# State-space heads taken two by two on both column halves of TensorE, the decay broadcast in one pass, another order on ScalarE and VectorE

## The reference

```
zxbcdt = u @ w_in                          # z 2048, x 2048, B 512, C 512, dt 32 columns
xbc = silu(causal_depthwise_conv(xbc, conv_w, conv_b))      # width 4
dt = softplus(dt + dt_bias); a = -exp(a_log); da = dt * a; xdt = xs * dt
a_cs = cumsum(da) inside a chunk of 128 positions
cb = C^T B per chunk and group
y_diag = (cb * exp(a_cs[l] - a_cs[s]), s <= l) @ xdt        # per head
states = B, decay_to_end, xdt -> per chunk; prev = scan over the 4 chunks
y_off = C @ prev * exp(a_cs)                                # per head
y = y_diag + y_off + d * xs;  y = y * silu(z);  y = rms_norm(y per group) * norm_w
out = y @ w_out
```

## Time and profile before

| what | value |
|---|---|
| median of the runs | 2882.8 us (2881.28 to 2891.03) |
| profiled execution, its own time | 2888.43 us |
| its span in the trace | 2886.6 us |
| mean granted TensorE clock | 0.988 of full speed |
| TensorE matmul busy | 2800.2 us, 97% |
| weight load busy | 2271.8 us, 79% |
| VectorE, ScalarE, GpSimd busy | 1727.6, 791.0, 1732.4 us |
| share of TensorE in the chain that ended last | 84% |
| SSD groups 0 to 3 in the trace | 1310.2 to 1601.5 us |

### The profile page before, as it was taken

The page is one execution under the profiler, slowest core; times in us unless marked ns, Lnnn a source line. Parts: engine busy times, 40 slices in busy tenths (PEclk is TensorE's granted clock), DMA queues, the critical chain, the costliest instruction groups (busy, mean ns, idle before and its releaser), DMA issues.

```text
span 2886.6 us, 37343 instructions
## 1 busy us (share of the span) xinstructions
PE 2800.2 (97%) x13446; PEld 2271.8 (79%) x13446; DVE 1727.6 (60%) x1974; ACT 791.0 (27%) x1299; POOL 1732.4 (60%) x984
## 2 busy tenths in 40 slices
PE   8899999999899999999998999999999998999999
PEld 6778888888787888877776778888877776788887
DVE  6886766427867665264665558054567776832635
ACT  3434222103443222025555322010222222310202
POOL 5784666666966666754443548666464443666664
PEclk9999999999999999999999999999999999999999
DMA  4201323332012223322111223222231211222321
GB/s 148 66 30 66 95 94 99 105 97 95 23 54 90 97 95 101 103 84 71 61 64 51 69 71 114 98 95 95 73 108 59 67 60 57 84 100 95 98 98 59
DMA packets 66484, 237.45 MB, mean 82 GB/s; under 512 B 7264, under 2 KB 7520, under 8 KB 66336
## 3 DMA queue, kind: packets, MB, share of 16 engines
q1 hardware_dynamic: 65504, 234.00, 24.8%
q10 hardware_dynamic: 832, 1.51, 0.2%
HBM read 233.38 MB, written 2.10 MB: 82 GB/s over the span
## 4 chain that ended last, share of the span: by engine, by line
PE 84%; DVE 8%; DVEq 3%; issue 3%; ACT 1%; POOL 0%; DMA 0%; ACTq 0%; SPq 0%; POOLq 0%
PE ps L476 25%; PE ps L482 24%; PE ps L479 24%; PE ps L1137 1%; DVE qw L2487 1%; PE ps L879 1%; PE ps L639 1%; DVE ps L1786 1%; PE ps L997 1%; PE ps L989 1%; PE ps L992 1%; PE ps L1173 1%; PE ps L882 1%; PE ps L957 0%; DVEq L1905 0%
## 5 line engine op out<-in xcount | busy, mean ns | idle before, releaser
L411 POOL TENSOR_SCALAR w_hi<-w_raw 128x1024 fp32r<-128x1024 f32 x437 | 482.1, 1103 | 1100.0 <-PE ps L476 1013.0
L413 POOL TENSOR_TENSOR w_lo<-w_raw,w_hi 128x1024 fp32r<-128x1024 f32 x437 | 1100.6, 2519 | 36.5
L476 PE MATMUL ps<-x_hi,w_hi 128*128 128x512 f32 x1864 | 746.2, 400 | 26.3 <-DVE x_lo L1658 5.3
L482 PE MATMUL ps<-x_hi,w_lo 128*128 128x512 f32 x1864 | 730.0, 392 | 0.0
L479 PE MATMUL ps<-x_lo,w_hi 128*128 128x512 f32 x1864 | 729.6, 391 | 0.0
L476 PEld LDWEIGHTS ps<-x_hi,w_hi 128*128 128x128 f32 x1864 | 352.4, 189 | 115.0 <-issue 14.0
L482 PEld LDWEIGHTS ps<-x_hi,w_lo 128*128 128x128 f32 x1864 | 352.2, 189 | 75.6
L479 PEld LDWEIGHTS ps<-x_lo,w_hi 128*128 128x128 f32 x1864 | 352.7, 189 | 74.4 <-issue 4.1
L476 PE MATMUL ps<-a_hi,w_hi 128*128 128x512 f32 x512 | 200.0, 391 | 0.0
L482 PE MATMUL ps<-a_hi,w_lo 128*128 128x512 f32 x512 | 199.2, 389 | 0.0
L479 PE MATMUL ps<-a_lo,w_hi 128*128 128x512 f32 x512 | 199.2, 389 | 0.0
(11 more groups left out here) (424 smaller groups left out, 4678.6 us busy)
## 6 DMA issues: line engine op xcount, KB each, us to landing
w_raw<-wts SPq DMA_DIRECT2D x437, 512.0 KB, 3.4
xres<-xT SPq DMA_DIRECT2D x2, 1024.0 KB, 8.3
outT<-xres SPq DMA_DIRECT2D x8, 256.0 KB, 2.1
pf<-pT ACTq DMA_DIRECT2D x2, 512.0 KB, 3.8
prm<-prm SPq DMA_DIRECT2D x1, 452.0 KB, 3.9
lev<-levels ACTq DMA_DIRECT2D x1, 384.0 KB, 3.9
wtmp<-pos SPq DMA_DIRECT2D x1, 128.0 KB, 3.2
ident<-identity SPq DMA_DIRECT2D x1, 64.0 KB, 10.1
```

The source lines that it names most:

```text
L411: nc.gpsimd.tensor_scalar(w_hi[:, s, :], w_raw[:, s, :], 1.0, 0.0, ALU.mult, ALU.add).then_inc(w_rounded[s], 1)
L413: nc.gpsimd.tensor_tensor(w_lo[:, s, :], w_raw[:, s, :], w_hi[:, s, :].bitcast(F32), ALU.subtract).then_inc(w_split[s], 1)
L476: mm = nc.tensor.matmul(out, whi, xhi, start=first, stop=False)
L482: return nc.tensor.matmul(out, wlo, xhi, start=False, stop=last)
```

## The change

`head_pair(g, p)` replaces two calls of `head`. It issues the same 14 matmuls for heads 2p and 2p+1, but in turn: the even head on the lower half of the columns, the odd head on the upper, for each chunk first the two `seg` products, then the two `ctu` products. `yh_done` counts pairs. `seg` and `ctu` have 4 buffers, and a decay waits for the pair two before it; to make room, `cs`, `csT`, `dtT`, `ident_r` and `aex` move to space that is free at that time.

`spread` is one matmul: `cs_hl` holds the rounded decay in rows 0 to 31 and its rest in rows 32 to 63, and column k of `ident_r` has a one in rows k and k + 32.

The order on TensorE: `spread(g, 1)` stands behind the first state product; a pair takes 4+4+4+4 steps in groups 1 and 2, 3+3+3+3 in group 0, 2+1+2+1 in group 3, with `spread(2p+2)`, `head_pair(p)` and `spread(2p+3)` between the four shares. The last pair of group 3 stands behind all steps.

On ScalarE `decays(g, 1)` comes right behind the copy of the first state, ahead of `norm_root`, and later decays come first at each r. On VectorE the order at each r is `pair`, `decayed(g, r + 1)`, `conv_sides`, and `group_norm` is spread over r = 1 to 4, the reciprocal at r = 1.

```diff
@@ -253,18 +253,17 @@ tiles
-        seg, _ = at("seg", [P, 2, S])
-        ctu, _ = at("ctu", [P, 2, S - P])
-        cs, _ = at("cs", [P, S])
-        cs_hi, _ = at("cs_hi", [P, S], F32R)
-        cs_lo, _ = at("cs_lo", [P, S], F32R)
-        csT, _ = at("csT", [P, TT, SH])
-        dtT, _ = at("dtT", [P, TT, SH])
+        seg, _ = at("seg", [P, 4, S])
+        ctu, _ = at("ctu", [P, 4, S - P])
+        cs_hl, _ = at("cs_hl", [P, S], F32R)
+        csT, _ = at("csT", [P, TT, SH], F32, o_rope + 640)
+        dtT, _ = at("dtT", [P, TT, SH], F32, o_rope + 1152)
...
-        ident_r, _ = at("ident_r", [P, SH], F32R)
-        aex, _ = at("aex", [P, 1])
+        cs, _ = at("cs", [P, S], F32, o_y + 5 * 2048)
+        ident_r, _ = at("ident_r", [P, SH], F32R, o_rope + 1664)
+        aex, _ = at("aex", [P, 1], F32, o_rope + 1792)
...
@@ -863,24 +862,26 @@
-                nc.tensor.matmul(ps[3][:, :], col, cs_hi[:, :], start=True, stop=False)
-                nc.tensor.matmul(ps[3][:, :], col, cs_lo[:, :], start=False, stop=True).then_inc(csb_done, 1)
-
-            def head(g, r):
-                k, p, r0 = GH * g + r, r // 2, (r % 2) * HD
-                out = ps[4 + p % 2]
-                pe.wait_ge(m_ready, k + 1)
-                if r == 0:
+                nc.tensor.matmul(ps[3][:, :], col, cs_hl[:, :], start=True, stop=True).then_inc(csb_done, 1)
+
+            def head_pair(g, p):
+                n, out = GT * g + p, ps[4 + p % 2]
+                pe.wait_ge(m_ready, 2 * n + 2)
+                if p == 0:
                     pe.wait_ge(xdt_ready, TT * (g + 1))
                     pe.wait_ge(h_ready, 2 * (g + 1))
-                if r % 2 == 0 and GT * g + p >= 2:
-                    pe.wait_ge(y_read, GT * g + p - 1)
+                if n >= 2:
+                    pe.wait_ge(y_read, n - 1)
+                both = [(r, slice((r % 2) * HD, (r % 2 + 1) * HD)) for r in (2 * p, 2 * p + 1)]
                 for tt in range(TT):
-                    mm = nc.tensor.matmul(out[r0:r0 + HD, tt * P:(tt + 1) * P], xdt[:, tt, r * HD:(r + 1) * HD],
-                                          seg[:, r % 2, tt * P:(tt + 1) * P], start=True, stop=tt == 0)
+                    c = slice(tt * P, (tt + 1) * P)
+                    for r, rows in both:
+                        mm = nc.tensor.matmul(out[rows, c], xdt[:, tt, r * HD:(r + 1) * HD], seg[:, r % 4, c],
+                                              start=True, stop=tt == 0)
                     if tt:
-                        mm = nc.tensor.matmul(out[r0:r0 + HD, tt * P:(tt + 1) * P], hst[:, tt - 1, r * HD:(r + 1) * HD],
-                                              ctu[:, r % 2, (tt - 1) * P:tt * P], start=False, stop=True)
+                        for r, rows in both:
+                            mm = nc.tensor.matmul(out[rows, c], hst[:, tt - 1, r * HD:(r + 1) * HD],
+                                                  ctu[:, r % 4, (tt - 1) * P:tt * P], start=False, stop=True)
                 mm.then_inc(yh_done, 1)
...
@@ -956,18 +957,26 @@
                     steps_of(ahead, some)
+                    if c == 0:
+                        spread(g, 1)
                     if c == 0 and g:
                         norm_sum(g - 1)
                         steps_of(ahead, some)
                 if g == 0:
                     steps_of(ahead, 1)
-                for r in range(GH):
-                    steps_of(ahead, (4 if g else 3) if some else 2)
-                    if r + 1 < GH:
-                        spread(g, r + 1)
-                    steps_of(ahead, (4 if g else 3) if some else 1)
-                    head(g, r)
-            steps_of(ahead, len(TILES) * KD)
+                for p in range(GT):
+                    share = [4 if g else 3] * 4 if some else [2, 1, 2, 1]
+                    steps_of(ahead, share[0])
+                    if p + 1 < GT:
+                        spread(g, 2 * p + 2)
+                    steps_of(ahead, share[1])
+                    if some or p + 1 < GT:
+                        head_pair(g, p)
+                    steps_of(ahead, share[2])
+                    if p + 1 < GT:
+                        spread(g, 2 * p + 3)
+                    steps_of(ahead, share[3])
+            head_pair(GROUPS - 1, GT - 1)
...
@@ -1432,14 +1441,14 @@
-                if k >= 2:
-                    act.wait_ge(yh_done, k - 1)
+                if k >= 4:
+                    act.wait_ge(yh_done, k // 2 - 1)
...
@@ -1495,12 +1504,15 @@
                 AC.activation(hst[:, 0, :], ps[6 + n % 2][:, :], ACT.Copy).then_inc(h1_ready, 1)
                 act.drain().then_inc(misc_free[n % 2], 1)
+                decays(g, 1)
                 if g:
                     norm_root(g - 1)
                     z_silu(g, 0)
                     if some:
                         z_silu(g, 1)
                 for r in range(GH):
+                    if 1 <= r < GH - 1:
+                        decays(g, r + 1)
                     if some:
                         if r >= 3:
                             center(g + 1, CONV_T[r - 3])
@@ -1511,8 +1523,6 @@
                     else:
                         for i in {3: (1,), 6: (2,)}.get(r, ()):
                             z_silu(g, i)
-                    if r + 1 < GH:
-                        decays(g, r + 1)
                     if r >= 2 and r % 2 == 0:
                         gated_square(g, r // 2 - 1)
             z_silu(GROUPS - 1, 3)
...
-            V.tensor_copy(ident_r[:, :], ident[:, 0:SH])
+            V.tensor_tensor(ident_r[:, :], ident[:, 0:SH], ident[:, SH:2 * SH], ALU.add)
...
-            V.tensor_tensor(cs_lo[:, :], cs[:, :], cs_hi[:, :].bitcast(F32), ALU.subtract).then_inc(small_dve, 1)
+            V.tensor_tensor(cs_hl[SH:2 * SH, :], cs[0:SH, :], cs_hl[0:SH, :].bitcast(F32), ALU.subtract).then_inc(small_dve, 1)
...
-                dve.wait_ge(yh_done, GH * g + 2 * p + 2)
+                dve.wait_ge(yh_done, n + 1)
...
-            def group_norm(g):
-                dve.wait_ge(root2_ready, g + 1)
-                V.reciprocal(rstd[:, :], root[:, :])
-                dve.drain()
-                for p in range(GT):
-                    n = GT * g + p
-                    V.scalar_tensor_tensor(y[:, n, :], y[:, n, :], prm[:, C_NW + n, :], rstd[:, :],
-                                           ALU.mult, ALU.mult).then_inc(y_norm, 1)
+                V.tensor_tensor(seg[:, r % 4, :], seg[:, r % 4, :], cb[:, :], ALU.mult)
+                V.tensor_tensor(ctu[:, r % 4, :], ctu[:, r % 4, :], cT[:, g % 2, P:], ALU.mult).then_inc(m_ready, 1)
+
+            def group_norm(g, p):
+                if p == 0:
+                    dve.wait_ge(root2_ready, g + 1)
+                    V.reciprocal(rstd[:, :], root[:, :])
+                    dve.drain()
+                n = GT * g + p
+                V.scalar_tensor_tensor(y[:, n, :], y[:, n, :], prm[:, C_NW + n, :], rstd[:, :],
+                                       ALU.mult, ALU.mult).then_inc(y_norm, 1)
...
@@ -2277,17 +2287,18 @@
                     dve.wait_ge(misc_done, n + 1)
                     V.tensor_tensor(hst[:, c, :], hst[:, c, :], ps[6 + n % 2][:, :], ALU.add).then_inc(h_ready, 1)
                     dve.drain().then_inc(misc_free[n % 2], 1)
+                decayed(g, 1)
                 for r in range(GH):
+                    if r >= 2 and r % 2 == 0:
+                        pair(g, r // 2 - 1)
+                    if 1 <= r < GH - 1:
+                        decayed(g, r + 1)
                     if g + 1 < GROUPS and r >= 3:
                         conv_sides(g + 1, CONV_T[r - 3])
-                    if r >= 2 and r % 2 == 0:
-                        pair(g, r // 2 - 1)
-                    if r + 1 < GH:
-                        decayed(g, r + 1)
                     if r in (5, 7):
                         add_squares(g, (r - 3) // 2)
-                    if r == 1 and g:
-                        group_norm(g - 1)
+                    if 1 <= r <= GT and g:
+                        group_norm(g - 1, r - 1)
             def y_lo_part(k):
                 dve.wait_ge(y_hi_ready, k + 1)
                 hi, lo = (x_hi[:, k, :], x_lo[:, k, :]) if k < 8 else (y2_hi[:, k - 8, :], y2_lo[:, k - 8, :])
@@ -2301,7 +2312,8 @@
             add_squares(GROUPS - 1, 3)
             for k in range(4, 12):
                 y_lo_part(k)
-            group_norm(GROUPS - 1)
+            for p in range(GT):
+                group_norm(GROUPS - 1, p)
             for k in range(12, DI // P):
                 y_lo_part(k)
 
```

More of the change, by code:

```diff
@@ L1434, in decays @@
                 act.wait_ge(csb_done, k + 1)
-                if k >= 2:
-                    act.wait_ge(yh_done, k - 1)
+                if k >= 4:
+                    act.wait_ge(yh_done, k // 2 - 1)
                 for tt in range(TT):
-                    AC.activation(seg[:, r % 2, tt * P:(tt + 1) * P], ps[3][:, tt * P:(tt + 1) * P], ACT.Relu,
```

(19 more changed lines are left out.)

## The result

The changed kernel takes 2866.0 us (median of 4 runs, 2861.11 to 2866.84) against 2885.6 us for the kernel before in the same comparison (4 runs). The ratio is 0.9926, 95% interval 0.9913 to 0.9939: 21.4 us faster, between 17.6 and 25.1. Forecast were 27.9 us. The sign and the stated range (2847 to 2869 us) held; the gain was forecast 6.5 us too large. The time itself lies 11 us above the 2855 us of the forecast, of which 2.8 us are the kernel before, whose median was 2882.8 us in the prediction and is 2885.6 us here.

What follows compares the result with a forecast made beforehand. TensorE's queue was taken to bound groups 0 to 2, a ScalarE and VectorE chain group 3. Gains of 28.0 less 3.1 us, plus 3 in group 3, gave 27.9 us off 2882.8: 2855 us, range 2847 to 2869.

Steps and rivals of the forecast that it cites:

- Column halves: Heads on TensorE: two heads on different column halves overlap, 1.67 us per pair, each pair saving 1.87 us with edges.
- Rivals A and C: Pairs on TensorE: A, column halves do not overlap, 2875 us, 6%; C, each half change costs a drain, 2915 us, 3%.
- Broadcast: Decay broadcast on TensorE: 32 second passes go, each worth 0.23 us, 7.4 us in all.
- Groups 1 and 2: Middle loops of heads, TensorE-bound: 9.3 us gained per group, less the new root wait of 1.5 us.
- the wait for the root: Last state product waits for ScalarE's root, delayed by decays(g, 1): 1.5 us, two groups 3.1 us, bounds 0 to 7.2.
- I charge nothing here: Groups 0 to 2, decay chain through ScalarE and VectorE feeding pairs: no cost charged, 0 to 14 us kept as range.
- rival B: Groups 0 to 2: VectorE or ScalarE becomes late, about 1.1 us wait per pair, giving back 13 us: 2868 us, 14%.
- Group 3: Last group, paced by a ScalarE and VectorE chain: 3 us gained with what follows, bounds -2 and +8.
- The hand-made schedule: Group 3 followed pair by pair: first pair starts 1565.2, second waits near 5 us, last ends 1599.1 against 1601.48 before.
- The own range: Whole kernel: 2848 to 2862 us, with the wait for the root and group 3 at their ends.

Runs made afterwards that it cites:

- e2: Changed kernel with all 7 matmuls of a pair's even head before the odd head's 7, not alternated: 11.8 us faster than the kernel before.
- e1: Kernel before with only the one-pass broadcast added, heads, buffers and order as before: 8.9 us faster than the kernel before.
- e8: Changed kernel with ScalarE's order root, decays(g,1), gate tiles: 22.2 us faster than the kernel before; groups 1 and 2 at 71.9 us each.
- e3: Changed kernel with ScalarE's norm root and gate tiles z0, z1 ahead of decays(g,1): 23.4 us faster than the kernel before.
- e10: Changed kernel with reordered ScalarE and VectorE work, later silu of B and C, later group 3 norm and gated squares: 2849.4 us, ratio 0.9867 against kernel before.
- e5: Changed kernel with GpSimd's subtraction cut to 128 columns for w_in blocks, other low parts left out: 38.7 us faster than the kernel before.
- e11: Changed kernel unmodified, run and profiled again (the second profile): ratio 0.9930, 20.2 us faster than the kernel before.
- e4: Changed kernel with VectorE's decayed(g, r+1) ahead of pair(g, r/2-1): 23.7 us faster than the kernel before.

## Why the prediction was right, and where it was off

*Column halves:* right. 1.68 us per pair measured, 1.67 forecast; e2 takes 1.15 us per pair of the gain away again. Rivals A and C are out. The reading of two existing rows, L1137 and L1150, carried to a moving operand twice as long and to accumulation. The rule of the Trainium skill on weight loads, which the prediction quotes against it from "TensorE: Matmul & The Clock Gate", section "Part 3: Packing small matmuls — row/col tiling", did not hold here: 28 loads for two heads on the same rows fitted into the 1.68 us.

*Broadcast:* right. 7.4 us forecast for 32 passes; 5.8 us in groups 0 to 2 of e1, where 24 of them give 5.6, and 8.0 with group 3.

*Groups 1 and 2:* right within 0.3 us. 7.8 us each forecast (9.3 less 1.5), 8.0 measured; the wait for the root was 1.20 us against 1.5, and without it (e8) a group gives 9.5. It is shown that the wait is real, and that it returns elsewhere if the root and the gate tiles both go ahead of the decay (e3). The pairs stand 13.3 us apart in group 1, 13.5 forecast.

*Groups 0 to 2, "I charge nothing here":* the term that failed, in group 0. It gave 3.2 us instead of 9.3 in the first profile and 7.0 in the second one. I had 1.4 us of slack for group 0 and put in a pair or nothing in front of a decay; the prices of VectorE were those of undisturbed instructions. The kernel before has stretched ones too: the mean of L2232 is 0.78 us where one alone takes 0.69, and a single one took 2.88. The mean of a group hides this: one hold costs 2.2 us in one piece, more than the slack, and the low clock behind the wait another 1.5. That is rival B, at one of three groups and with another mechanism than the one I gave it: VectorE is not full, it is held. The condition was worked out and the price was not. How much it costs is chance: 6.1 us of the 9.3 in the first profile, 2.3 in the second.

*Group 3:* over-estimated. 3 us were forecast with what follows; the group gave 0.4, and in the second profile it was 1.1 us longer than before. The 2.4 us behind it are no more than that stretch varies by (3.1 us between the two profiles), so that 2.8 us came together against 3 is luck. The hand-made schedule was close in its places (waits of 4.7 and 2.1 us at the second and fourth pair, worked out as near 5 and 2.5; the last pair ended 59.5 us behind the group's start, 58 forecast), but it missed that `decayed(3,1)` and `decayed(3,3)` each meet a subtraction: 2.72 and 2.84 us instead of 0.55 and 0.69. The first pair waited 1.67 us behind the first of them and started 26.3 us into the group, where the schedule had 23.6; all later pairs kept about that delay. How much of it is the hold, no run shows. That the group is a chain through two engines and not bound by TensorE was right, and e10 shows that 9.2 us can be had there without touching TensorE's work, in the one profile that there is.

Sum, forecast against the first profile: group 0 9.3 and 3.2, groups 1 and 2 together 15.6 and 16.1, group 3 with what follows 3 and 2.8, ahead of the groups 0 and -0.4. The shortfall is group 0 in this profile; in the second one the groups gave 22.0 us, 2.3 short in group 0 and about 4 in group 3. The own range of 2848 to 2862 us, which moved only the root and group 3, was missed by 4 us: 2866.0 is inside the stated range because rival B, at 2868, had widened it. e5, in which GpSimd's subtraction is short in groups 0 to 2 and ahead of them, gains 17 us more than the changed kernel, but 7.4 of these lie ahead of group 0 and some behind group 3; for the cause only its group lengths are used.

## What to carry to other kernels

Here matmuls with 64 output channels cost nothing for the second head when they were written in turn on the two column halves (1.68 us for two heads, 1.67 for one). To learn that beforehand, look for two lines of different alternation in the profile and compare their starts. When TensorE is made faster, price the feeding engines at their slowest instruction, not at their mean: here a VectorE multiplication with two SBUF inputs was held for nearly the whole length of a GpSimd subtraction, and whether it was depended on 0.05 us. Keep more slack than one such hold (here 2.2 us) between what feeds TensorE and its use: groups 1 and 2 had it and lost nothing, group 0 had 1.4 us. Compare profiles stretch by stretch, and take a second profile of the same kernel before giving a difference a cause.

## What the runs showed of the hardware that was not expected

TensorE runs matmuls of different column halves side by side even where they are not written in turn: in e2 at the boundary of two heads, starts 0.05 us apart instead of 0.11, 0.35 us saved per pair. The seven held VectorE multiplications ended 0.4 to 0.6 us behind GpSimd's subtraction, and the holding goes both ways: in e11 GpSimd's rounding took 1.60 us instead of 1.05 while VectorE multiplied. After waits of 3.31 and 4.72 us the pair began at half the clock (8 instructions in 1.12 us), after waits of 0.99 and 2.13 us at the full one (0.66). The wait just before does not decide it alone: in e4, after 3.28 us, a pair began at the full clock and fell to half on its way, and in e11 the third pair of group 3 waited 0.66 us and ran at a granted clock of 0.52, in 3.1 us.
